# Two edits at the entry to the expert passes: where one broadcast row is computed, and how many weight halves are asked for first

## The reference

```
mod = c_act @ ada_w[i] + ada_b[i]
shift1, scale1, gate1, shift2, scale2, gate2 = jnp.split(mod[:, None, :], 6, axis=-1)
...
h = rms_norm(x, norm2_g[i]) * (1.0 + scale2) + shift2
y = moe_swiglu(h, moe_router[j], moe_w1[j], moe_w3[j], moe_w2[j])   # top 2 of 8 experts
x = x + gate2 * y
```

## Time and profile before

| what | value |
|---|---|
| median of 3 runs | 1376.8 us (1372.06 to 1377.62) |
| the profiled execution's own time | 1371.17 us |
| its span, first to last instruction | 1369.4 us |
| mean granted TensorE clock | 0.992 |
| PE busy | 1308.8 us, 96% |
| DVE, ACT busy | 916.8 us, 739.3 us |
| HBM read | 472.46 MB |

### The profile page before, as it was taken

The page is one execution under the profiler, slowest core; times in us unless marked ns, Lnnn a source line. Parts: engine busy times, 40 slices in busy tenths (PEclk is TensorE's granted clock), DMA queues, the critical chain, the costliest instruction groups (busy, mean ns, idle before and its releaser), DMA issues.

```text
span 1369.4 us, 20765 instructions
## 1 busy us (share of the span) xinstructions
PE 1308.8 (96%) x8030; PEld 957.1 (70%) x8030; DVE 916.8 (67%) x1526; ACT 739.3 (54%) x1273; POOL 10.5 (1%) x45
## 2 busy tenths in 40 slices
PE   7999999999999999999999999998999999789986
PEld 5875899999888988567748888836845773157521
DVE  4688899888887658577849998908936760067401
ACT  4655654444475557567629998807825750057200
POOL 0000000000000020000000000000000000000000
PEclk9999999999999999999999999999999999999999
DMA  8985758889757257999999999999999969999997
GB/s 320 383 316 206 271 216 307 314 293 331 282 181 286 88 192 279 409 419 406 421 414 416 408 413 413 422 394 414 411 419 410 421 262 387 422 404 421 386 419 297
DMA packets 130146, 474.92 MB, mean 347 GB/s; under 512 B 9437, under 2 KB 11626, under 8 KB 107514
## 3 DMA queue, kind: packets, MB, share of 16 engines
q1 hardware_dynamic: 128672, 472.28, 88.1%
q10 hardware_dynamic: 1370, 1.25, 0.3%
HBM read 472.46 MB, written 1.05 MB: 346 GB/s over the span
## 4 chain that ended last, share of the span: by engine, by line
PE 74%; DMA 11%; DVE 9%; ACT 2%; SPq 2%; issue 1%; DVEq 0%; ACTq 0%
PE bank L1793 10%; PE bank L1796 10%; PE bank L1794 10%; DMA ring<-in_moe_w 7%; PE bank L1896 5%; PE bank L1327 3%; PE bank L1330 3%; PE bank L1326 3%; PE bank L1620 2%; PE bank L1890 2%; PE bank L1707 2%; PE bank L1024 2%; SPq L868 2%; PE bank L1370 2%; PE bank L1368 2%; PE bank L1074 2%
## 5 line engine op out<-in xcount | busy, mean ns | idle before, releaser
L3241 DVE TENSOR_TENSOR lo_third<-ring,hi_third 128x512 fp32r<-128x512 f32 x164 | 107.6, 691 | 28.0 <-ACT hi_third L2378 27.3
L2378 ACT ACTIVATE hi_first<-ring 128x512 fp32r<-128x512 f32 x156 | 96.2, 631 | 53.6 <-DMA ring<-in_moe_w 35.8
L3241 DVE TENSOR_TENSOR lo_first<-ring,hi_first 128x512 fp32r<-128x512 f32 x156 | 102.3, 691 | 29.8 <-ACT hi_first L2378 29.4
L3241 DVE TENSOR_TENSOR lo_second<-ring,hi_second 128x512 fp32r<-128x512 f32 x160 | 104.6, 691 | 14.1 <-ACT hi_second L2378 13.5
L2378 ACT ACTIVATE hi_third<-ring 128x512 fp32r<-128x512 f32 x164 | 101.1, 632 | 22.1 <-PE bank L1796 13.9
L2378 ACT ACTIVATE hi_second<-ring 128x512 fp32r<-128x512 f32 x160 | 98.9, 631 | 22.9 <-PE bank L1796 17.2
L2655 DVE SCALAR_TENSOR_TENSOR ada_acc<-ring,c_act,ada_acc 128x512 f32<-128x512 f32 x140 | 105.1, 751 | 3.9
L1896 PE MATMUL bank<-ring,work 128*32 128x512 f32 x648 | 86.9, 595 | 7.8 <-DMA ring<-in_moe_w 7.3
L2009 ACT ACTIVATE w_hi<-ring 128x1024 fp32r<-128x1024 f32 x66 | 68.7, 1053 | 46.1 <-PE bank L1375 23.4
L2890 DVE TENSOR_TENSOR w_lo<-ring,w_hi 128x1024 fp32r<-128x1024 f32 x66 | 79.3, 1221 | 9.8 <-ACT w_hi L2009 9.6
L1326 PE MATMUL bank<-hg_hi,w_hi 128*128 128x256 f32 x336 | 82.7, 284 | 0.0
(11 more groups left out here) (566 smaller groups left out, 3278.9 us busy)
## 6 DMA issues: line engine op xcount, KB each, us to landing
ring<-in_moe_w SPq DMA_DIRECT2D x208, 1024.0 KB, 18.9
ring<-in_ada_w SPq DMA_DIRECT2D x24, 2048.0 KB, 12.3
ring<-in_moe_w SPq DMA_DIRECT2D x44, 768.0 KB, 16.1
ring<-in_ffn_w SPq DMA_DIRECT2D x15, 2048.0 KB, 9.0
beside_x<-in_moe_w SPq DMA_DIRECT2D x17, 1024.0 KB, 18.9
beside_out<-in_moe_w SPq DMA_DIRECT2D x17, 1024.0 KB, 19.0
beside_h<-in_moe_w SPq DMA_DIRECT2D x16, 1024.0 KB, 18.9
beside_w<-in_moe_w SPq DMA_DIRECT2D x15, 1024.0 KB, 20.6
```

Source lines behind the costliest of these rows:

```text
L2378: A(hi_piece(Q), raw_piece(SPLITS[r], q, j), ACT.Copy).then_inc(hi_done, 1)
L3241: v.tensor_tensor(lo_piece(Q), raw_piece(SPLITS[r], q, j), hi_piece(Q).bitcast(F32), ALU.subtract).then_inc(lo_done, 1)
```

## The change

- The eight matmuls that spread gate2 move from pass 0 to the last norm, where they stand in the place of two `keep_pace` matmuls. They write banks 0 and 1 in place of 4 and 5. The ACT copies to `g2bc` move behind the copies of `h_rows`.
- The remaining two `keep_pace` calls, and the matmuls that count tokens for each expert, use banks 6 and 2 in place of 0 and 1. PE waits for one `h_rows` copy (`s_hth`) before the counts, and for `s_g2e` at the start of pass 0, not in `gather(1)`.
- `ahead` has 20 halves, not 17, so slots 8 and 9 of pass 0 are complete in it. SP waits for `s_places` behind ask 19, not behind ask 16. There are still 17 homes, so asks 17 to 19 wait for uses 0 to 2.

```diff
-    GAIN_AT = 5
...
+    FIRST_HALVES = 20
...
-    ahead = [(0, n // 2, n % 2) for n in range(len(HOMES))]
+    ahead = [(0, n // 2, n % 2) for n in range(FIRST_HALVES)]
...
                 load_expert_half(sp, ids[m], KINDS[m], i, h, n)
-                if n == len(HOMES) - 1 or (m, h) == (0, 1) and i >= PER - NE + 2:
+                if n == FIRST_HALVES - 1 or (m, h) == (0, 1) and i >= PER - NE + 2:
...
-            keep_pace(2, 0)
+            pe.wait_ge(s_dg, 1)
+            for k in range(KT):
+                last = mm(psum[k // 4][:, (k % 4) * P:(k % 4 + 1) * P], ones[:], diag[:, k, :], start=True, stop=True)
+            last.then_inc(s_g2, 1)
...
-            keep_pace(1, 0)
+            keep_pace(1, 6)
...
-            mm(psum[1][:, 0:NE], ones[:], selT[:, 0, :], start=True, stop=False)
-            mm(psum[1][:, 0:NE], ones[:], selT[:, 1, :], start=False, stop=True).then_inc(s_pos, 1)
-            keep_pace(1, 0)
+            pe.wait_ge(s_hth, 1)
+            mm(psum[2][:, 0:NE], ones[:], selT[:, 0, :], start=True, stop=False)
+            mm(psum[2][:, 0:NE], ones[:], selT[:, 1, :], start=False, stop=True).then_inc(s_pos, 1)
+            keep_pace(1, 6)
...
-                if g == 1:
-                    pe.wait_ge(s_g2e, 1)
...
+                            else:
+                                pe.wait_ge(s_g2e, 1)
...
-                    if q == GAIN_AT and m == 0:
-                        pe.wait_ge(s_dg, 1)
-                        for k in range(KT):
-                            last = mm(psum[4 + k // 4][:, (k % 4) * P:(k % 4 + 1) * P], ones[:], diag[:, k, :],
-                                      start=True, stop=True)
-                        last.then_inc(s_g2, 1)
...
+            act.wait_ge(s_g2, 1)
+            for g in range(2):
+                last = A(g2bc[:, g * 512:(g + 1) * 512], psum[g][:, :], ACT.Copy)
+            last.then_inc(s_g2e, 1)
...
-                    if q == GAIN_AT + 1 and m == 0:
-                        act.wait_ge(s_g2, 1)
-                        for g in range(2):
-                            last = A(g2bc[:, g * 512:(g + 1) * 512], psum[4 + g][:, :], ACT.Copy)
-                        last.then_inc(s_g2e, 1)
...
-            link(v.tensor_copy(counts, psum[1][:, 0:NE]))
+            link(v.tensor_copy(counts, psum[2][:, 0:NE]))
```

## The result

The changed kernel takes 1378.1 us (median of 22 runs, 1375.3 to 1386.1), the kernel before 1375.7 on the same chips (22 runs, 1372.1 to 1379.0). The ratio is 1.0025, with a 95% interval of 1.0015 to 1.0036: +3.4 us, from 2.1 to 5.0. (The ratio is estimated from all runs and is not the quotient of the two medians, which are 2.4 apart. Wherever this text gives a difference of run times with a sign, it comes from the ratio.) I had forecast +3.1, and 1380 on a median of the kernel before that was 1.1 above the one measured here. By the bound of 0.5% that is no change, but the interval excludes zero: the change costs a little.

The account below looks back on a forecast made before the run. PE (96% busy) and DMA (11%) were read as limits taking turns, with landed halves as slack. Lateness 4.6 - 1.1 = +3.5, less 0.4, gave +3.1 (ACT's 0.05 inside): 1376.8 + 3.1 = 1380 rounded, range 1373.5 to 1385.

Parts of the forecast that it names:

- Fills out, gate2 matmuls in, copies in: Last norm: swapping fills for gate2 matmuls costs 0; ACT's copies, hidden by its idle 1.08 us, cost 0.05 us.
- PE's 1.4 at gather(1): End of pass 0's gate2 work: without those matmuls PE starts gather(1) 1.4 us earlier, bounds 0 and -1.8.
- Head start worth 0: Asks 17 to 19 go earlier, but asks 20 to 23 keep their gates, so the time gains 0.
- Shift of the DMA stream: From asks 23 and 25 on, the DMA stream runs 1.6 us earlier, bounds -1.4 and -2.1.
- Lateness of slot 7's last half: Pass 1: this half, now ask 35, lands at 579.0, so PE starts on it 4.6 us later.
- The wait at slot 12 gives back 1.1: Pass 0, at 625.85: PE's 1.11 us wait behind an ACT copy goes, leaving 4.6 - 1.1 = +3.5.
- 0.4 less at 893: At 893 to 898 the DMA engines had run dry; 0.4 us of lateness is absorbed, bounds 0 and 1.5.
- Rival C: PE's waits before 579 bring a clock dip: +4.6, or +6 if DVE eats the 1.4; 1381.5 to 1383; 25%.
- Rival B: Light halves land in time after all, so only PE's 1.4 us shows: 1375; 10%.
- Rival D: New order fills dry DMA moments around ask 23; pass 1 late by 2, net 0 to +1: 1377.3; 10%.

Follow-up runs that it names:

- gate2 alone: The changed kernel with 17 halves first in place of 20, so only the gate2 matmuls, copies and banks move: 1373.26 us, ratio 0.9991 to the kernel before.
- 18 first: Changed kernel with 18 halves first, not 20: 1372.85 us, ratio 0.9985; with ACT's silu of pass 1's chunk 1 ahead of slot 12 too: 1374.39, 0.9991.
- The weave: The changed kernel with pass 1's light slots 4, 6 and 7 used later, behind pass 0's slots 5 and 6: 1373.16 us, ratio 0.9991 to the kernel before.
- 20 first and the early silu: The changed kernel with ACT's silu of pass 1's chunk 1 put ahead of pass 0's slot 12: 1377.50 us, ratio 1.0028 to the kernel before.
- 19 first: The changed kernel with 19 halves first in place of 20: 1377.12 us, ratio 1.0016 to the kernel before.
- 23 first: The changed kernel with 23 halves first in place of 20: 1392.64 us, ratio 1.0142 to the kernel before.

## Why the prediction came out right, step by step

The forecast of the time was +3.1 and the runs have +3.4, from 2.1 to 5.0. An agreement to 0.3 inside an interval 2.9 us wide is luck; what can be checked is the chain of steps.

- *Fills out, gate2 matmuls in, copies in.* Forecast 0 and 0.05; measured 0 and under 0.02. The idle 1.08 us hid 1.10 us of copies.
- *PE's 1.4 at gather(1).* Measured 1.2: 535.79 less 521.15, against 536.38 less 520.53. The step held, a little short. In the time it is worth -1.2 (from -3.2 to +0.7), and by the pass 2 mark only 0.3 of it survives the wait at slot 12.
- *Head start worth 0.* Right, shown twice: ask 20 did not move, and a kernel that knows pass 1's number gains nothing that can be measured.
- *Shift of the DMA stream.* Forecast -1.6. Ask 25 landed 1.4 earlier, relative, and ask 56 landed 1.0 earlier. This term was 0.6 too large. With gate2 alone ask 56 gained only 0.4: asks 23 and 24 took 6.6 and 7.2 us to land there, 5.0 in the changed kernel. All traces of kernels that ask the halves in the order before (17 first, with the number waited for) have 6.3 to 7.2, but 18 first has 5.3 and 5.0 in one trace and 7.0 and 6.7 in another. Why is open.
- *Lateness of slot 7's last half.* Forecast 4.6; measured 579.97 - 574.40 - 0.62 = 4.95. The error is that of the stream: in the times of the kernel before, the half was to land at 579.0 and landed at 579.3 (579.9 - 0.62).
- *The wait at slot 12 gives back 1.1.* Right: 4.95 - 1.11 = 3.84, and the mark has 3.78. The weave shows that this chain is the cause and not only in step with it.
- *0.4 less at 893.* Not seen. Pass 4 starts 899.87 - 893.64 - 0.62 = 5.6 later, not 3.1. The window there says why:

```profile
895.80:902.60 6.80, 6.80 (x30) 3.79 (x33) 0.00 (x0) 0.38 (x1) 0.00 (x0) 0.50 0.08 32
```

  Half clock from 895.8, that is (899.87 - 895.8) / 2 = 2.0 us of lost work, and 5.6 - 2.0 = 3.6. The kernel with 20 first and the early silu has no such stretch there, and its pass 4 starts 3.8 later. So 0.4 was too much; 0 is nearer. From the reference event to the end of the span it is 4.7 later in the changed kernel and some 5 in the other, in the runs 3.4. How the last passes take up the difference is not shown.
- *Rival C* had the right place for part of this. PE's waits in slot 4 were followed by half clock from 564.7 to 568.1. But what PE lost there only shortened its waits in slot 7, where it starts at the landing of ask 35 in any case, so the pass 2 mark owes it nothing. With 19 first the half clock came behind the last of the waits, and with 23 also in the first light stretch; there it counted.
- *Rival B* needed ask 35 by 573; it landed at 579.9. *Rival D* needed the dry moments to be filled; at 540 to 545 they grew, from 329 to 259 GB/s.

Beyond the sizes, one sentence was not right: that PE's instructions have a fixed order "so it has no way to make this up". Within the kernel as written that is so. The weave shows that the order itself is the cheap thing to move.

The Trainium skill's page "DMA: Bandwidth & Descriptors", section "Rules for kernel authors", says to issue a DMA early and wait late. Here issuing early, taken alone, cost from 4.7 us (the ratios 1.0025 and 0.9991, of the changed kernel and of gate2 alone) to 6.9, since with 17 homes and one queue each half asked early pushes another back. The second half of the rule, wait late, is what the weave adds, and both together give 1373.2 and 1371.7 (ratios 0.9991 and 0.9976).

## What to carry to other kernels

Where homes are limited and one queue serves all, a head start only changes the order: count in transfers how much later the displaced half lands (here 6.5 us for three halves: 58.8 against 572.8 - 520.5 = 52.3), and set against it its slack (here 1.6 us) and the wait that stands downstream (here 1.1); what exceeds both is the cost. An idle gap in a DMA rate is no gain by itself; ask whether the next request waits for the queue or for a home. If the asks must be reordered, reorder the uses with them, and check the next place where an in-order engine stands on a DMA with another engine's copy behind it: a gain upstream ends there.

## What the runs showed of the hardware

- Half clock (1.2 of 2.4 GHz) came behind some of PE's waits in the light stretches: from within the wait of 3.16 us on, PEclk was 0.50 for 10.2 us (23 first), and behind waits of 1.39 and 1.42 us it was 0.51 for 3.4 us (19 first). It does not follow from such a wait alone: behind the wait of 1.33 with 18 first, and behind 0.18 and 1.41 in slot 7 of the changed kernel, the clock stayed full. Three traces have it without any wait, for 3.4 us at the end of gather(1) (from 540.4, 538.1 and 538.4). A light half at half clock takes 1.94 us, not 1.07. PE's busy time rose by 4.3 us in the changed kernel, with the same work.
- Such stretches go with the noise between runs: in profiles of near-identical kernels they come at 708, 889, 891 or 930 us, in lengths of 3.4 or 6.8 us, and each 3.4 us of them takes 1.7 us of PE's work. Over the 22 runs of the changed kernel, from a mean clock of 0.992 down to 0.981, the time rises by 0.8 us for each 0.001 that the clock falls (correlation -0.8). So the end of a single profile can't tell 2 us. A mark inside it can, as far as no such stretch lies ahead of it.
- A half of 1 MB, asked when nothing else was under way, took 5.0 us (ask 17 of the changed kernel), but ask 23 of the kernel before took 6.7, with the half ahead of it 2.0 us from landing.
